# Fetching an expert's rows by indirect transfers in place of one-hot matrix products

## The reference, cut to what matters

```python
def moe_swiglu(h, w_router, w_gate, w_up, w_down):
    logits = jnp.einsum('bsd,de->bse', h.astype(F32), w_router.astype(F32))
    top_val, top_idx = lax.top_k(logits, TOP_K_EXPERTS)          # 2 of 8
    top_w = jax.nn.softmax(top_val, axis=-1)
    combine = jnp.sum(jax.nn.one_hot(top_idx, N_EXPERTS, dtype=F32) * top_w[..., None], axis=-2)
    out = jnp.zeros_like(h)
    for e in range(N_EXPERTS):
        out = out + combine[..., e:e + 1].astype(h.dtype) * swiglu(h, w_gate[e], w_up[e], w_down[e])
    return out
```

## Time and profile before

| | |
|---|---|
| time, median of 3 runs | 1975.77 us (1973.17 to 1976.76) |
| the profiled execution: its time | 1981.63 us |
| its span, first to last instruction | 1979.8 us |
| PE busy | 1875.7 us (95%) |
| PE weight loads (PEld) busy | 1526.8 us (77%) |
| DVE busy | 1436.7 us (73%) |
| ACT busy | 1124.0 us (57%) |
| POOL busy | 358.2 us (18%) |
| moved by DMA | 494.89 MB, mean 250 GB/s |

### The profile page before, as it was taken

The page is one execution under the profiler, slowest core; times in us unless marked ns, Lnnn a source line. Parts: engine busy times, 40 slices in busy tenths (PEclk is TensorE's granted clock), DMA queues, the critical chain, the costliest instruction groups (busy, mean ns, idle before and its releaser), DMA issues.

```text
span 1979.8 us, 26486 instructions
## 1 busy us (share of the span) xinstructions
PE 1875.7 (95%) x9005; PEld 1526.8 (77%) x9005; DVE 1436.7 (73%) x1635; ACT 1124.0 (57%) x1303; POOL 358.2 (18%) x299
## 2 busy tenths in 40 slices
PE   7899999999999997999998879999999999999996
PEld 6677886767887775788787568888888888888884
DVE  5748774557875685645568458989898989898896
ACT  5744433654443464434446446767676767676774
POOL 3722113552102463100146200000000000000000
PEclk9999999989999999999999879999999999999998
DMA  7339984327987331555533349989898989898992
GB/s 263 106 135 349 345 316 160 118 97 289 351 311 258 108 112 43 196 187 190 190 119 113 128 142 360 371 317 381 323 376 317 382 316 382 313 385 313 382 358 95
DMA packets 234828, 494.89 MB, mean 250 GB/s; under 512 B 23016, under 2 KB 74432, under 8 KB 228608
## 3 DMA queue, kind: packets, MB, share of 16 engines
q1 hardware_dynamic: 225664, 492.91, 69.4%
q10 hardware_dynamic: 8768, 0.65, 0.3%
q0 software_dynamic: 320, 0.36, 0.2%
HBM read 492.77 MB, written 1.10 MB: 249 GB/s over the span
## 4 chain that ended last, share of the span: by engine, by line
issue 45%; PE 42%; DVE 7%; ACT 3%; POOL 1%; DMA 1%; SPq 0%; DVEq 0%; POOLq 0%; ACTq 0%
PE bank L2277 13%; PE bank L2279 12%; PE bank L2278 12%; DVE slab L1228 1%; ACT slab L1978 1%; PE bank L2716 1%; POOL w_lo L815 1%; PE bank L2487 1%; PE bank L2396 1%; ACT w_hi L1828 1%; PE bank L2465 1%; DMA slab<-in_w_mlp_out 1%; PE bank L2447 1%; DVE w_lo L920 0%; DVE x L1017 0%
## 5 line engine op out<-in xcount | busy, mean ns | idle before, releaser
L920 DVE TENSOR_TENSOR w_lo<-slab,w_hi 128x2048 fp32r<-128x2048 f32 x369 | 846.9, 2304 | 245.0 <-ACT w_hi L1828 244.6
L1828 ACT ACTIVATE w_hi<-slab 128x2048 fp32r<-128x2048 f32 (+2 forms) x421 | 796.8, 1899 | 366.8 <-PE bank L2279 283.8
L2277 PE MATMUL bank<-w_hi,hT_hi 128*128 128x512 f32 (+3 forms) x1664 | 651.8, 392 | 20.2 <-DVE w_lo L920 6.0
L2279 PE MATMUL bank<-w_hi,hT_lo 128*128 128x512 f32 (+3 forms) x1664 | 641.1, 385 | 0.0
L2278 PE MATMUL bank<-w_lo,hT_hi 128*128 128x512 f32 (+3 forms) x1664 | 640.9, 385 | 0.0
L2277 PEld LDWEIGHTS bank<-w_hi,hT_hi 128*128 128x128 f32 x1664 | 318.0, 191 | 83.9 <-DVE w_lo L920 10.5
L2279 PEld LDWEIGHTS bank<-w_hi,hT_lo 128*128 128x128 f32 x1664 | 317.2, 191 | 60.4
L2278 PEld LDWEIGHTS bank<-w_lo,hT_hi 128*128 128x128 f32 x1664 | 317.9, 191 | 56.0
L815 POOL TENSOR_TENSOR w_lo<-slab,w_hi 128x512 fp32r<-128x512 f32 (+2 forms) x208 | 262.3, 1296 | 384.5 <-ACT w_hi L1828 364.8
L2277 PE MATMUL bank<-w_hi,hid_hi 128*128 128x512 f32 x680 | 267.7, 394 | 3.7 <-DVE hid_lo L1497 3.7
L2279 PE MATMUL bank<-w_hi,hid_lo 128*128 128x512 f32 x680 | 266.7, 392 | 0.0
(11 more groups left out here) (243 smaller groups left out, 1302.4 us busy)
## 6 DMA issues: line engine op xcount, KB each, us to landing
slab<-in_w_exp_gate SPq DMA_DIRECT2D x176, 512.0 KB, 5.6
slab<-in_w_exp_up SPq DMA_DIRECT2D x176, 512.0 KB, 5.5
slab<-in_w_exp_down SPq DMA_DIRECT2D x176, 512.0 KB, 5.4
slab<-in_w_ada SPq DMA_DIRECT2D x48, 1024.0 KB, 5.0
slab<-in_w_mlp_in SPq DMA_DIRECT2D x64, 512.0 KB, 6.6
slab<-in_w_mlp_out SPq DMA_DIRECT2D x64, 512.0 KB, 6.2
slab<-in_w_in SPq DMA_DIRECT2D x56, 512.0 KB, 4.8
slab<-in_w_out SPq DMA_DIRECT2D x32, 512.0 KB, 4.5
```

The source lines that it names most:

```text
L920: dve.tensor_tensor(w_lo[:, q, 0:n], raw(s)[:, 0:n], w_hi[:, q, 0:n].bitcast(F32), ALU.subtract).then_inc(lo_dve, 1)
L1828: act.activation(w_hi[:, q, 0:n], raw(s)[:, 0:n], ACT.Copy).then_inc(hi_done, 1)
L2277: pe.matmul(dst, a_hi, b_hi, start=start, stop=False)
L2279: return pe.matmul(dst, a_lo, b_hi, start=False, stop=stop_)
```

## The change

Two internal DRAM tensors are new. `h_rows` holds the 256 normalised rows and 128 spare rows; ACT writes it once, by two transfers, before the experts. `y_rows` (384 rows) takes the outputs; POOL clears it once, also before the experts. The one-hot matrix is still made, but PE multiplies it by only two columns (token number and router weight, `list_places`), and DVE makes from the two sums a column of 128 row numbers in `index` and a column of weights in `listw` (`make_index`). Empty list places get the numbers of spare rows, so that each transfer always moves 128 rows of 4 KB.

- **In:** POOL fetches the rows of expert n+1 from `h_rows` by an indirect transfer (`fetch`). PE transposes them (`turn_fetched`, 8 transposes) ahead of the last step of expert n, and ACT and DVE split them there. The product `gather` is left for the first expert alone.
- **Out:** ACT copies the finished output with the router's weight as its scale into `y_out`. POOL adds it into rows of `y_rows` by an indirect, accumulating transfer (`scatter` on POOL). The scatter product on PE, the split by DVE and the four additions by DVE are gone for all experts but the last.
- **Waits:** `make_index` overwrites the column of row numbers that the transfer of the output of expert n-1 reads, so DVE waits for that transfer (`scattered`). POOL's fetch stands behind it in POOL's queue.
- **The end:** `fold` moves to POOL, which reads the sums back from `y_rows` (a 1 MB transfer) once seven experts are added, during the last expert. DVE no longer has it.
- **Order at the ends:** in the first expert ACT and DVE split one more tile ahead of the first silu (`ahead`); in the last step of the last expert one of the two tiles is split ahead of the hidden columns, where both stood behind them.

```diff
+            def fetch(p, n, n0):
+                pool.wait_ge(ix_made, 2 * n + 2)
+                pool.wait_ge(ga_done, n)
+                pool.indirect_dma_start(fetched, None, h_rows, bass.IndirectOffsetOnAxis(index[p][:, 0:1], 0)).then_inc(rows_in, 16)
+            def scatter(p, n, n0):
+                pool.wait_ge(yo_done, 2 * (n - n0 // NE) + 2)
+                pool.wait_ge(scattered, 16 * (n + 1))
+                pool.indirect_dma_start(y_rows, bass.IndirectOffsetOnAxis(index[p][:, 0:1], 0), y_out, None, compute_op=ALU.add
+                                        ).then_inc(scattered, 16)
+            def fold(turn_):
+                pool.wait_ge(scattered, 16 * NE * (turn_ + 1))
+                pool.dma_start(acc, y_rows[0:SEQ].rearrange("(t p) d -> p t d", p=P)).then_inc(acc_in, 16)
+                pool.wait_ge(row_in, 16 * (2 * DEPTH + 1))
+                pool.wait_ge(acc_in, 16 * (turn_ + 1))
+                for t in range(TT):
+                    pool.tensor_tensor(acc[:, t, :], acc[:, t, :], rowg[:, :], ALU.mult).then_inc(fold_done, 1)
+                for t in range(TT):
+                    pool.wait_ge(fold_done, 4 * turn_ + 1 + t)
+                    pool.tensor_tensor(x[:, t, :], acc[:, t, :], x[:, t, :], ALU.add).then_inc(fold_done, 1)
...
+                def make_index(p, n, old):                                        # DVE
+                    dve.wait_ge(ix_t, n + 1)
+                    if old:
+                        dve.wait_ge(scattered, 16 * n)
+                    dve.tensor_scalar(unlisted[:, :], bank[6][:, 0:1], 0.0, place[:, 0:1], ALU.is_equal, ALU.mult).then_inc(ix_un, 1)
+                    dve.tensor_copy(listw[:, p:p + 1], bank[6][:, 1:2]).then_inc(ix_made, 1)
+                    dve.wait_ge(ix_un, n + 1)
+                    dve.scalar_tensor_tensor(index[p][:, :], bank[6][:, 0:1], float(SEQ), unlisted[:, :], ALU.add, ALU.add
+                                             ).then_inc(ix_made, 1)
...
-                        step(0)
-                        if not first:
-                            output_low(n - 1)
+                        step(0, ahead=int(first))
+                        if last:
+                            last_lists(n)
+                        else:
+                            lists(2 * i + p + 1, n + 1)
+                        step(1, ahead=1)
                         if not last:
-                            lists(2 * i + p + 1, n + 1)
-                        step(1, between=(lambda: None) if first else lambda: add_output(2 * i + p - 1, n - 1))
-                        if not last:
-                            listed_rows((p + 1) % 2, n + 1)
-                        expert_steps(dve, ring, lambda j: step(j, not (last and isinstance(j, int))))
+                            make_index(1 - p, n + 1, not first)
+                        expert_steps(dve, ring, lambda j: step(j, not (last and isinstance(j, int))),
+                                     lambda: None if last else listed_rows(1 - p, n + 1))
...
-                            act.activation(ye_hi[:, c * COL:(c + 1) * COL], bank[2 + c][:, :], ACT.Copy
-                                           ).then_inc(ye_done, 1)
+                            act.activation(y_out[:, c * COL:(c + 1) * COL], bank[2 + c][:, :], ACT.Copy, scale=listw[:, p:p + 1]
+                                           ).then_inc(yo_done, 1)
...
+                def list_places(n):                                               # PE
+                    pe.wait_ge(g_done, 3 * n + 3)
+                    for t in range(TT):
+                        ins = pe.matmul(bank[6][:, 0:2], scr(X_G + t * P, P), tokw[:, t, :], start=t == 0, stop=t == TT - 1)
+                    ins.then_inc(ix_t, 1)
+                def turn_fetched(n, n0):
+                    pe.wait_ge(rows_in, 16 * (n - n0 // NE))
+                    for k in range(KC):
+                        ins = pe.transpose(bank[4 + k // 4][:, (k % 4) * P:(k % 4 + 1) * P], fetched[:, k * P:(k + 1) * P], ident)
+                    ins.then_inc(ga_done, 1)
...
                         rows_up(1)
                         if not first:
-                            scatter(1 - p, n - 1)
+                            pe.wait_ge(yo_done, 2 * (n - n0 // NE))
                         sums(n, 0, True, False)
                         turn(1)
-                        if not last:
-                            gather(n + 1)
+                        if last:
+                            turn_last_list(n)
+                        else:
+                            list_places(n + 1)
```

More of the change, by code:

```diff
@@ L241, in build @@
         flag = sb("flag", [1, 1], I32)
+        listed_cols = sb("listed_cols", [P, 8])
+        tokw = listed_cols[:, 0:2 * TT].rearrange("p (t c) -> p t c", t=TT)
+        place, unlisted, listw = listed_cols[:, 4:5], listed_cols[:, 5:6], listed_cols[:, 6:8]
+        index = [posi[:, i:i + 1] for i in range(2)]
         def k_(name, *shape):
@@ L275, in build @@
         mods = nc.dram_tensor("mods", (DEPTH, NROW, COL), F32, kind="Internal").ap()
+        h_rows = nc.dram_tensor("h_rows", (SEQ + P, D), F32, kind="Internal").ap()
+        y_rows = nc.dram_tensor("y_rows", (SEQ + P, D), F32, kind="Internal").ap()
         w_loaded = [sem(f"w_loaded{i}") for i in range(6)]
@@ new lines, in expert_rows @@
+            def expert_rows(n0):
+                for n in range(n0, n0 + NE):
+                    p = n % 2
+                    if n > n0:
+                        scatter(1 - p, n - 1, n0)
+                    if n < n0 + NE - 1:
+                        fetch(1 - p, n + 1, n0)
+                fold(n0 // NE)
+            pool.wait_ge(acc_zero, 1)
+            clear_sums()
+            pool.wait_ge(rows_out, 32)
+            expert_rows(0)
+            pool.wait_ge(flag_done, 1)
+            full = pool.value_load(flag[0:1, 0:1], min_val=0, max_val=SEQ + 1)
@@ L897, in _ @@
+            with pool.If(full > P + 1):
+                pool.wait_ge(fold_done, 4)
+                pool.memset(big[:, 0:D], 0.0).then_inc(acc_zero, 1)
+                pool.wait_ge(acc_zero, 2)
+                clear_sums()
+                expert_rows(NE)
             root(0, TT)
@@ L1675, in body, with step @@
                         expert_ring(ring, i, p, t0, loads0)
-                        def step(j, more=True, between=None):
+                        def step(j, more=True, ahead=0):
                             at = ub + n * MS + j
@@ L1680, in step @@
                             if isinstance(j, int) and j == MS - 1:
-                                late = 2
-                            if not more:
-                                fold(n)
-                            if between:
+                                late = 2 if more else 1
+                            late -= ahead
+                            for _ in range(ahead):
                                 lo()
-                                late = 3
                             dve.wait_ge(act_done, at + 1)
@@ L2213, in step @@
                                     hi()
-                            step(0, te + (2 if first else 0))
+                            step(0, te + (2 if first else 0), ahead=int(first))
                             if not first:
-                                output(n - 1, te + 2)
-                            step(1, te + 6)
-                            if not last:
-                                listed_rows((p + 1) % 2, n + 1)
-                            expert_steps(act, ring, lambda j: step(j, te + 6 * j - 1, not (last and isinstance(j, int))))
+                                output(1 - p, n - 1, te + 2)
+                            step(1, te + 6, ahead=1)
+                            if last:
+                                last_listed(n0 // NE)
+                            expert_steps(act, ring, lambda j: step(j, te + 6 * j - 1, not (last and isinstance(j, int))),
+                                         lambda: None if last else listed_rows(1 - p, n + 1))
                         listed_rows(0, n0)
@@ L2845, in body @@
                             sums(n, MS - 2, False, False, lambda: turn(MS - 1))
+                        else:
+                            turn_fetched(n + 1, n0)
+                            rows_up(MS - 1)
+                            sums(n, MS - 2, False, False)
+                            turn(MS - 1)
                     if n0 == 0:
```

141 lines of the change are left out of this document (64 added, 77 removed).

## The result

The changed kernel took 1929.0 us (median of 4 runs, 1921.0 to 1934.3) against 1974.5 us of the kernel before (4 runs, 1972.2 to 1976.8): ratio 0.9765, 95% interval 0.9741 to 0.979, so 45.5 us less, 41 to 51 by the interval. I had said 1936, 1922 to 1968. Two later comparisons of the same pair gave 0.9773 (0.9751 to 0.9795) and 0.9762 (0.9738 to 0.9787). The profiled execution took 1921.01 us, its span is 1919.2 us.

What follows compares the result with a forecast made beforehand. PE was taken to bind the kernel, with DVE and transfers close behind. 38.7 - 4.2 - 3.7 + 3.0 + 6.6 = 40.4 us off the profiled 1981.6; for the median, 1936 us was forecast, range 1922 to 1968.

Steps and rivals of the forecast that it cites:

- likeliest case: Whole kernel: PE sets the period without scatter and gather, time 1926 to 1946 us; 56 in 100.
- PE's row: PE's instructions in each expert: 6.81 us leave, 1.16 enter, floor 93.6 us; 38.7 us gained over seven gathers and scatters.
- Transfers, -4.2 us: Seven experts: fetch and addition raise the transfers' need to 93.7 us, so stalls lose 0.6 us per expert.
- I read this as their ceiling: Transfer engines: 386 GB/s with a deep backlog taken as their limit, so the weights need 89.6 us of each period.
- The wait for `scattered`: `make_index` on DVE waits for the previous output's addition: about 14 us to land, 18.1 available, cost nothing.
- Fold on POOL, -3.7 us: Last expert: four POOL operations slow DVE's `lo`, which falls 4.7 us behind with 1 us of lead; 3.7 us lost once.
- First expert, +3.0 us: Narrow turn: one more tile split before the silu removes most of PE's 3.23 us idle time; 3.0 us gained.
- Last expert, +6.6 us: End of the kernel: without the fold on DVE the last sums start at 1952.0 instead of 1958.62; 6.6 us gained.
- third rival: Whole kernel: the change is cheaper still, with free small products, hidden fold and no stall; 1922 to 1926 us, 5 in 100.
- rival of the binding transfers: Expert period: the two row transfers cost 8.2 us, so an expert takes 97.8; 1946 to 1967 us, 20 in 100.
- harder form: Transfers in the middle experts: a mixed-traffic ceiling of 359 GB/s leaves gains only at the ends; 1970 us, 4 in 100.
- rival of the held DVE: `make_index` in six experts: slow accumulating transfer holds DVE, 2007 us if landing takes 30 us; 10 in 100.

Runs made afterwards that it cites:

- the two runs: The changed kernel with one and with three more accumulating transfers of 0.52 MB an expert: 1934.72 us and 1965.86 us.

## Why the prediction was right, point by point

The time lay 7 us under my 1936, inside the range, and by the likeliest case: PE's row shortens, the transfers stay hidden. That it came so near is in part luck. The transfers had been charged 4.2 us too much, and the fold 1.8 to 2.3 too little.

- **PE's row.** Predicted floor 93.6 us, measured 93.73. Of the 5.65 us an expert 5.52 came. The next wide matmul comes 1354.19 - 1353.39 = 0.80 us after the transposes, 0.35 of them the transposes' own, so the small products cost 0.45 where I took 0.46:

```profile
1353.39 0.60 PE L2462 MATMUL bank<-const,slab 128*128 128x128 f32 x4
1353.82 0.51 PE L2827 MATMUL bank<-listed_cols,slab 128*128 128x2 f32 x4
1354.19 0.48 PE L2343 MATMUL bank<-w_hi,hT_hi 128*128 128x512 f32 x1
```

  The eight transposes cost 0.87 where I took 0.70 (1404.23 to 1405.45 us, less 0.35). The split between gather and scatter was less good: the gather's part is 2.72 (predicted 4.58 - 0.52 - 0.70 = 3.36), the scatter's, with its wait and the small products, 2.80 (2.23 + 0.52 - 0.46 = 2.29). In the run with the gather kept it costs 3.58 us of PE's row (1417.91 to 1421.84, less 0.35), and 3.58 - 0.87 is the 2.72 to a hundredth. My 4.58 also held the transposes of the one-hot matrix (L2762), which belong to the scatter. Seven times 5.52, less the 0.9 of the first gather, is 37.7 in place of 38.7.
- **Transfers, -4.2 us.** Mis-sized: nothing. The step that failed is "I read this as their ceiling": 386 GB/s was the rate of a stretch in which they did not bind the kernel, and 394 is what they gave where they did, and with loads and one fetch alone in another stretch. Without the row transfers the period is the same, 93.74. The price of an accumulating transfer, 2.7 against 2.54 as the two runs give it, was about right.
- **The wait for `scattered`.** Cost nothing, as said. Its deadline of 18.1 us was 1273.09 - 1254.75 = 18.3, its landing 11.0 us after the copy and not 14.
- **Fold on POOL, -3.7 us.** Mis-sized: 5.5 to 6.0 (74.8 to 75.3 less 69.3). I had scaled one row of DVE from 512 to 1024 columns. The whole-instruction rule was the better model: 4.4 us a tile and 5.8 in all, against the 4.35 to 4.40 at which PE got its tiles. The granted clock stayed at 1.00 there.
- **First expert, +3.0 us.** Mis-sized: 4.1, since the wait also cost clock, and 5.3 between the two profiled executions (19.95 less 14.69).
- **Last expert, +6.6 us.** From the first half of the sums to the last sums it now takes 5.5 us (1892.34 to 1897.85) in place of 12.0, so 6.5 came. But I had put all of it on the fold. With the fold on DVE and the rest of the new order it takes 10.1 (from 1898.0, 4.13 and the last matmul ahead of 1902.49, to 1908.10): 1.9 us are the order of the last tiles and 4.6 the fold. The expectation of that run had 12.0 or 5.5, and neither came. Moving the fold to POOL gained 4.6 and cost 5.5 to 6.0. By the traces that part of the change is a loss of about 1 us; the medians (1928.0 with the fold on DVE, 1928.2 to 1929.0 as changed) can't show it.

With the measured terms the sum is 37.7 + 0 - 5.5 + 4.1 + 6.5 = 42.8 us, or 42.3 with a fold of 6.0, against 45.5 in the medians (41 to 51). The two profiled executions can be compared more closely. Of their 48.0 us in the experts, 4.4 lie ahead of the narrow turn (34.9 less 30.5) and I ascribe them to the execution, since changed kernels show both values; whether the kernel before has both too I can't say from its one trace. That leaves 43.6. The sum with the 5.3 of the first expert in place of 4.1 is 44.0. So the traces leave nothing open beyond half a microsecond, and the medians up to 3 us.

One sum of the prediction is wrong as written. In the third rival, 3.7 - 0.5 stands where the first expert's 3.0 belongs; the time it gives moves by 0.2 us.

The rival of the binding transfers needed more than 1.7 us an expert beyond what they cost. The harder form, 359 GB/s, stands against 378 to 383 in every stretch of the middle and 394 at the limit; the 358 of the Trainium skill (DMA: Bandwidth & Descriptors, Specifications) is no limit for this one core. The rival of the held DVE was nearer than its price suggested, 7.4 us; the step from there on would have been 1.16 us for each us.

## What to carry to other kernels

A ceiling read from a busy stretch is a lower bound: only a run in which the transfers bind gives the ceiling, and two such runs with different extra work give price and ceiling at once. Work that is moved to another engine to free one isn't free for it if they exclude each other, as DVE's splits and POOL's operations did here: it is paid on both sides, and small pieces placed in the idle time of the engine that is nearly full can be cheaper than any move. A wait whose deadline is met costs nothing until it isn't; then it can cost more than its length, as here 10.9 us for 9.4, because PE's granted clock fell behind the stop.

## What was not expected of the hardware

- The transfers sustained 394 GB/s when an accumulating transfer is counted as read and written. The indirect fetch of 128 rows of 4 KB landed after 7.5 us with 0.98 us of POOL for its issue, the accumulating one after 10.5 us with 2.36; a direct load of the same size took 6.8 to 7.3 beside them.
- The granted clock was 0.66 in the 5 us that hold the end of a stop of PE of 3.2 us, and 0.60 in the ten that hold the end of one of 6.7 us.
- An operation of 512 columns on POOL took 1.3 to 3.4 us by where it fell between DVE's tiles, and DVE lost 0.8 to 1.0 for each.
